# Two row gathers issued together, and the clearing of weight buffers moved behind them

## The reference, cut to what matters

```python
scores = jax.nn.sigmoid(xt @ w_router)
_, top_idx = lax.top_k(masked, TOP_K)            # 8 of 64 experts for each token
...
def expert_block(acc, blk):                      # tokens sorted by expert, in blocks
    tok, g, e = blk
    xb = xt[tok]
    hb = jax.nn.silu(xb @ w_e_gate[e]) * (xb @ w_e_up[e])
    yb = (hb @ w_e_down[e]) * g[:, None]
    return acc.at[tok].add(yb), None
```

## Time and profile before

| | us |
|---|---|
| median of 3 runs | 1871.96 |
| lowest and highest | 1871.76, 1872.28 |
| span of the profiled execution | 1868.7 |
| PE busy | 1743.7 (93%) |
| DVE busy | 1363.6 (73%) |
| ACT busy | 904.5 (48%) |
| POOL busy | 798.3 (43%) |

### The profile page before, as it was taken

How to read it: one execution, slowest core, us unless ns; L and a number is a source line. 1 busy time by engine, 2 the same in 40 slices (tenths; PEclk the granted TensorE clock), 3 DMA queues, 4 the chain that set the end, 5 groups by cost and what they waited for, 6 DMA issues and landing times.

```text
span 1868.7 us, 32562 instructions
## 1 busy us (share of the span) xinstructions
PE 1743.7 (93%) x8044; PEld 1402.5 (75%) x8045; DVE 1363.6 (73%) x1593; ACT 904.5 (48%) x1097; POOL 798.3 (43%) x658
## 2 busy tenths in 40 slices
PE   7899999998899999878999989999999999999997
PEld 5788888886788777657777777777777777777786
DVE  7999999914865347848677878777778778777554
ACT  5110011023600223457666767666667667666665
POOL 3357677753655450044344434434433444444100
PEclk9999999998999999889999999999999999999999
DMA  4111112221233443389888999999889999987532
GB/s 151 51 45 46 55 45 79 101 96 62 104 126 120 135 148 106 132 286 362 247 279 247 313 329 294 295 290 331 274 238 325 295 314 308 316 271 224 156 105 76
DMA packets 118199, 363.39 MB, mean 194 GB/s; under 512 B 23696, under 2 KB 40208, under 8 KB 109968
## 3 DMA queue, kind: packets, MB, share of 16 engines
q1 hardware_dynamic: 70608, 276.58, 40.6%
q0 software_dynamic: 28608, 69.55, 16.3%
q10 hardware_dynamic: 18944, 16.78, 2.7%
HBM read 323.98 MB, written 76.85 MB: 214 GB/s over the span
## 4 chain that ended last, share of the span: by engine, by line
PE 59%; issue 10%; DVE 10%; ACT 6%; DMA 6%; ACTq 1%; POOLq 1%; POOL 1%; DVEq 1%; SPq 0%
PE bank L123 10%; PE bank L124 10%; PE bank L125 10%; DMA xg<-h_rows,cur 4%; PE bank L1126 4%; DVE dn_lo L1872 3%; PE bank L1132 3%; PE bank L1127 3%; ACT gu_hi L1446 3%; PE bank L1103 3%; PE bank L1102 3%; PE bank L1107 3%; PE bank L1208 2%; PE bank L1206 2%; PE bank L1207 2%
## 5 line engine op out<-in xcount | busy, mean ns | idle before, releaser
L1867 DVE TENSOR_TENSOR gu_lo<-gu_raw,gu_hi 128x1024 fp32r<-128x1024 f32 x260 | 307.7, 1224 | 27.8 <-ACT gu_hi L1446 26.1
L815 POOL DMA_INDIRECT acc_rows<-y,cur x98 | 181.7, 1854 | 332.3 <-ACT y L1442 309.6
L123 PE MATMUL bank<-x_hi,w_hi 128*128 128x512 f32 x768 | 302.9, 394 | 11.6 <-ACTq L1280 6.3
L125 PE MATMUL bank<-x_hi,w_lo 128*128 128x512 f32 x768 | 300.1, 391 | 0.0
L124 PE MATMUL bank<-x_lo,w_hi 128*128 128x512 f32 x768 | 300.0, 391 | 0.0
L1591 DVE SCALAR_TENSOR_TENSOR bank<-a_buf,c_w_dw,bank 128x1024 f32<-128x1024 f32 x232 | 276.8, 1286 | 0.0
L1446 ACT CAST gu_hi<-gu_raw 128x1024 fp32r<-128x1024 f32 x260 | 260.4, 1055 | 0.0
L1102 PE MATMUL bank<-gu_hi,xh 128*128 128x512 f32 x512 | 206.1, 402 | 0.0
L1103 PE MATMUL bank<-gu_lo,xh 128*128 128x512 f32 x512 | 201.1, 393 | 0.0
L1107 PE MATMUL bank<-gu_hi,xl 128*128 128x512 f32 x512 | 195.1, 401 | 0.0
L1126 PE MATMUL bank<-dn_hi,hth 128*128 128x512 f32 x392 | 160.9, 411 | 28.3 <-DVE dn_lo L1872 23.5
(11 more groups left out here) (316 smaller groups left out, 3306.1 us busy)
## 6 DMA issues: line engine op xcount, KB each, us to landing
gu_raw<-in_w_gu SPq DMA_DIRECT2D x256, 512.0 KB
dn_raw<-in_w_dn SPq DMA_DIRECT2D x64, 1024.0 KB
w_raw<-in_w_mix SPq DMA_DIRECT2D x60, 512.0 KB, 3.4
acc_t<-acc_rows SPq DMA_DIRECT2D x16, 512.0 KB, 5.1
first_x<-in_x SPq DMA_DIRECT2D x8, 512.0 KB, 8.0
ga_d<-stage ACTq DMA_DIRECT2D x8, 512.0 KB, 2.6
gb_d<-stage ACTq DMA_DIRECT2D x8, 512.0 KB, 2.6
gb_in<-gb_d SPq DMA_DIRECT2D x8, 512.0 KB, 4.1
```

The source lines that it names most:

```text
L123: nc.tensor.matmul(o, wh[:, cols], x_hi[:, k, t], start=(i == 0), stop=False)
L125: last = nc.tensor.matmul(o, wl[:, cols], x_hi[:, k, t], start=False, stop=(i == len(ks) - 1))
L1867: nc.vector.tensor_tensor(gl[s][:, w], rg[s][:, w], gh[s][:, w], ALU.subtract).then_inc(gu_split, 1)
```

## The change

Six edits. (1) `xg[1]` is cleared early, behind `xg[0]`, once the two tiles that it overlaps are read for the last time (waits for `gs_made` 2 and `chosen`); the small tile `m1` is moved next to `before` so that only these two stand in the overlap. (2) POOL then waits for a new semaphore `plan_made`, which DVE raises behind the last write of the plan, and reads expert 1's first block into a register. (3) After the table is made, gather 0 takes block 0 as a constant and gather 1 follows directly. (4) Behind both stand the clearings of `dh[1]`, `dl[1]` and `xg[2]`, in this order. (5) The plan of expert 0 is read for the second block's gather, as before. (6) PE waits for `emptied` 4 (the four clearings up to `dl[1]`) in the place of `cleared` 2.

```diff
-    before, ramp, own = small("before", GROUPS * GROUPS), small("ramp", LISTS + 1), small("own", 1)
-    m1, m2, dup, g_score, g_keep, g_pen = (small(n, E) for n in ("m1", "m2", "dup", "gsc", "keep", "pen"))
+    before, m1 = small("before", GROUPS * GROUPS), small("m1", E)
+    ramp, own = small("ramp", LISTS + 1), small("own", 1)
+    m2, dup, g_score, g_keep, g_pen = (small(n, E) for n in ("m2", "dup", "gsc", "keep", "pen"))
...
             nc.gpsimd.memset(xg[0][:], 0.0).then_inc(emptied, 1)
+            pool.wait_ge(gs_made, 2)
+            pool.wait_ge(chosen, 1)
+            nc.gpsimd.memset(xg[1][:], 0.0).then_inc(emptied, 1)
+            pool.wait_ge(plan_made, 1)
+            second = plan_of(pool, 1)[0]
...
             pool.wait_ge(table_made, 1)
-            pool.wait_ge(emptied, 1)
-            gather(0, plan_of(pool, 0)[0], picked, 1)
-            nc.gpsimd.memset(xg[1][:], 0.0).then_inc(emptied, 1)
             pool.wait_ge(emptied, 2)
-            gather(1, plan_of(pool, 1)[0], picked, 2)
+            gather(0, 0, picked, 1)
+            gather(1, second, picked, 2)
+            nc.gpsimd.memset(dh[1][:].bitcast(F32), 0.0).then_inc(emptied, 1)
+            nc.gpsimd.memset(dl[1][:].bitcast(F32), 0.0).then_inc(emptied, 1)
             nc.gpsimd.memset(xg[2][:], 0.0).then_inc(emptied, 1)
-            pool.wait_ge(emptied, 3)
+            pool.wait_ge(emptied, 5)
             with pool.If(plan_of(pool, 0)[1] > 1):
                 gather(2, 1, picked_x, 1)
-            nc.gpsimd.memset(dh[1][:].bitcast(F32), 0.0).then_inc(cleared, 1)
-            nc.gpsimd.memset(dl[1][:].bitcast(F32), 0.0).then_inc(cleared, 1)
...
-            pe.wait_ge(cleared, 2)
+            pe.wait_ge(emptied, 4)
...
             step(v.tensor_copy(plan[:, :, 2], count[:]))
+            dve.sem_inc(plan_made, 1)
```

More of the change, by code:

```diff
@@ L536, in build @@
         scattered = [sem(f"scattered{q}") for q in range(3)]
-        cleared, emptied = sem("cleared"), sem("emptied")
+        plan_made, emptied = sem("plan_made"), sem("emptied")
         lows_kept, folded = sem("lows_kept"), sem("folded")
```

## The result

The changed kernel took 1862.59 us (median of 5 executions, 1860.40 to 1863.54), beside 1871.96 for the kernel before; the ratio is 0.9948 with an interval of 0.9933 to 0.9962, so 9.4 us or 0.5% less. The forecast of 1866.5 had the sign, but gave 5.4 us, and the result lies under the range that began at 1864.2. Over all executions of the two whole kernels but the three shown ahead of the prediction, the mean is 1870.9 before (118 executions, 1865.7 to 1880.2) and 1863.0 after (35 executions, the five above among them; one more, which took 3425.8 us, is left out): 7.9 us, with a standard error of 0.5. That mean lies under the range, too. The three shown ahead of the prediction had agreed within 0.6 us by luck: the next two were 1867.94 and 1875.89.

The account below looks back on a forecast made before the run. POOL's chain from the table to `dl[1]`'s clearing was taken to bound 790 to 811 us; 3.6 + 1.8 = 5.4 us off the 1868.7 span gives 1863.3, plus 3.3 to the median: 1866.5 us, range 1864.2 to 1870.6.

Parts of the forecast that it names:

- The wait for the clearing: At PE's loop entry: without waiting for `dl[1]`'s clearing, second flips come at 807.55, bound by `xl`, not 811.18: 3.6 us gained.
- The first gather: Behind the table on POOL: gather 0 issues earlier without register work, gaining 1.8 us, bounds 0 and 2.4 by its copy.
- The second gather hidden by 0.9 to 1.4 us: Ahead of the second flips: gather 1 lands before they want it at 805.75, the narrowest cover; rival that it waits, 0.19.
- Edits at nothing: On POOL and DVE: early `xg[1]` clearing, plan wait, extra increment and later gathers cost nothing; expert 2's gather about 4.8 us earlier.
- The clock: Rival at the flips: PE's clock stays up, both flip groups take 1.03 not 1.94 us; 2.4 us more, 1864.1; chance 0.10.
- The loop keeps it: In the experts' loop: no loss of the 5.4 us; rival that it takes gain back to 0 to 2, chance 0.14.
- The sum: Over the whole kernel: 3.6 + 1.8 = 5.4 us off the profiled span of 1868.7, median 1866.5 us.

Follow-up runs that it names:

- e3: Kernel before with only the two clearings of the down weights moved ahead of the clearing of xg[2] and the second block's gather: 1867.6 ± 0.6 us, ratio 0.9982.
- e1: Kernel before, run again unchanged: 1871.5 ± 0.5 us.
- e13: Kernel before, unchanged, a third profile with full traffic: 1871.5 ± 1.0 us.
- e5: Kernel before with a third of the experts' weight traffic left out from expert 2 on (output not the reference's): 1859.4 ± 0.5 us.
- e7: Changed kernel with six more clearings of xg[2] on POOL behind the table, ahead of both gathers: 1870.3 ± 0.6 us.
- e10: Changed kernel with a third of the weight traffic left out and 20 and 14 added PE transposes around the first flips: 1850.2 ± 1.1 us.
- e2: Changed kernel, run again unchanged: 1863.4 ± 1.0 us (10 executions).
- e6: Changed kernel with a third of the experts' weight traffic left out from expert 2 on: 1851.5 ± 0.8 us.
- e9: Changed kernel with a third of the experts' weight traffic left out, run again: 1852.1 ± 0.9 us.
- e16: Changed kernel with six more clearings of xg[2] ahead of both gathers, run again: 1869.9 ± 0.7 us.

## Why the prediction was right or wrong

**The wait for the clearing, 3.6 us, and what is late next: the mechanism held, the size failed.** With both changes the flips were released by `xl` (PE had waited for 2.57 us), PE's entry was done before, and the second gather was there. For the clearing alone `xl` isn't next: e3 shows gather 1 there, at 809.1. But 3.6 us is what this wait costs in the one profile that the forecast had. It is the time by which the second flips come later than `xl` allows (0.15 us behind its end, as in the changed kernel: 805.23 - 805.08). In the four profiles of the kernel before it is:

| profile | clearing done, behind the table | wait for it, beyond `xl` |
|---|---|---|
| first | 18.7 | 3.6 |
| e1 | 20.0 | 5.3 |
| e13 | 20.8 | 6.3 |
| e5 | 19.3 | 4.7 |

The mean is 5.0 us. This is the term that was mis-sized; the two loads of the plan and the copy for gather 1, shown above, make the difference.

**The first gather, 1.8 us with bounds 0 and 2.4:** the middle had been taken, and nearly the upper end came. The copy took 0.19 us in every profile of the changed kernel, and DVE's pair began at 790.70, after it, not within 0.05 us of it as I had read from the old trace. The instruction started 1.47 us behind the table in the place of 3.78, 2.3 us sooner, and the first flips 2.4. By the Trainium skill, page "SBUF — State Buffer", section "Who interferes with whom", whichever issues first gets the shared pair for the whole instruction. The trace agrees as far as the copy goes, which started first and wasn't prolonged (0.19 us). DVE's pair starts 0.71 us behind the table here and 0.36 in the earlier trace rows, but that can't be put down to the copy: in e7, where the copy comes only at 797.5, DVE waits just as long, and its cause stays open:

```profile
791.54 2.36 DVE L1875 TENSOR_TENSOR gu_lo<-gu_raw,gu_hi 128x1024 fp32r<-128x1024 f32 x2 [0.71 <-DVE table L1830]
```

With 2.3 in the place of 1.8 the second flips come at 805.2, as measured. The mean of all profiles gives 2.3 for the first flips, too.

**The second gather hidden by 0.9 to 1.4 us:** right. The packets of the two gathers pass one behind the other, as POOL's DMA queue shows for 796.5 to 800.5 us and for 800.5 to 804 (packets, MB, share):

```profile
q0 software_dynamic: 144, 0.56, 35.5%
...
q0 software_dynamic: 144, 0.55, 38.3%
```

The second is over by 804 and `xl` ends at 805.08, so the cover was about 1 us. In e10, where the flips could have gone sooner, it was the wait.

**Edits at nothing:** right in what they cost. `xg[1]` was cleared at 756.8 with POOL idle on both sides. Gather 2 was not sooner but equal (804.13 against 804.03), because the load of the plan ahead of it took longer: POOL was idle 2.60 us ahead of the copy, 1.70 in the earlier trace rows. The gather for expert 2 came 3.3 us sooner (813.73 and 810.39) in the place of 4.8, for the same reason. Both cost nothing.

**The clock:** the rival had 0.10. In the first profile the clock fell at 799 and both flips ran slow, but in e2, e6 and e9 the first flips came soon enough and took 1.09 us. Here are the windows of e2:

```profile
799.00:801.00 2.00, 1.09 (x8) 0.86 (x8) 0.00 (x0) 0.12 (x2) 0.07 (x1) 1.00 1.01 416
...
801.50:805.00 3.50, 1.48 (x7) 1.51 (x8) 1.35 (x3) 0.50 (x1) 2.13 (x3) 0.52 1.04 421
```

The second flips were slow in all six. What I had left out is that the way back can take longer, too: PE was at half clock for 4 us behind the start of the second flips of the changed kernel (805.2 to 809.2), for 3.1 before (811.2 to 814.3). A microsecond more at half clock is half a microsecond of PE's work, which is the 0.5 us between 5.95 and 5.48. Over all profiles the short first flips give 0.4 us in the mean (three of six), and from the second flips to the first write it takes 0.6 us longer (14.6 in the place of 14.0). So the rival came half, in half of the profiles, and the slower return took that back.

**The loop keeps it:** shown by e7 and e16, 7.1 ± 0.6 us for a delay of 6.9.

**The sum, and what failed.** By the means of the profiles it is 2.3 for the first gather, 0.4 for the first flips at the full clock, 5.0 for the clearing and 0.6 lost behind the second flips: 7.1 us in the place of 5.4, and this is what the starts give (36.3 in the mean of four before, 29.2 in the mean of six after). Most of the miss is the clearing's term, 5.0 in the place of 3.6: the durations of one profile were taken as those of the kernel, and of four that profile had the quickest path to the clearing. That the first pair of profiles shows 5.45, so near to the forecast, is no test of this term: its profile of before is the one that the terms were read from. Second, the lower end of the range, 1864.2, had nothing for the spread of a single comparison: executions of one kernel lie within 13 to 15 us (standard deviation 2.4 before, 2.8 after), and the base of 1871.96 was 1.1 above the mean of 118. Mean against mean it is 7.9 ± 0.5: 7.1 by the start, and 0.8 for which no cause is shown. With the error of the four starts (0.4) that rest is hardly clear of nothing; the mean loops of the profiles differ by 1.4 us, with whole traffic only, and the time behind the last write but one varies from 132.2 to 134.4 us in either kernel.

## What to carry to other kernels

When a wait on the path is removed, its worth is read from several profiles of the kernel before, not from one: a path made of many small steps on one engine varied by 2 us here, and the first trace was at its short end. Issue the transfers on which the others hang as soon as their indices stand, with all that can be prepared (cleared buffers, registers) behind earlier work, and look which of the removed waits hide each other: clearing and gathers gave 3.3 ± 0.6 and 3.2 ± 1.1 us alone, 7.9 ± 0.5 together. Before a range is given for an effect of 0.3%, more executions than three are wanted.

## What the runs showed of the hardware that was not expected

- A load of four integers of the plan into POOL's registers took 0.54 to 0.55 us in all 18 profiles in the time before DMA filled (784 to 792 us), and 0.58 to 1.67 us in all 20 cases between 794 and 803 us, in which DMA was full. Full DMA alone isn't the cause: the load for the second block's gather, 1.48 us at 800.5 in the changed kernel, takes 0.33 us in e3, where it comes at 804.2 with a DMA share of 1.15, and the loads in the loop of the kernel before, here up to 896 us with DMA share 1.00 from 850 on the earlier trace rows, take 0.32 to 0.34:

```profile
L557 POOLq TENSOR_LOAD <-plan x14: 319/328/338, 813.7 to 895.8; - x14
```

  What lengthens it ahead of 803 us stays open.
- The end of the kernel moved 1 to 1 with a delay of 6.9 us ahead of the loop (e7, e16), although DMA was 0.92 busy over the loop.
- PE's clock came back 3.1 us behind the second flips' start in the first profile of before and 4 us in that of the changed kernel, with PE busy from there on in both, and 4.9 us in e2; it fell 2.1 us after PE's last product in the changed kernel's first profile, 3.6 us after it in the kernel before.
